# Products with the identity written as transposing instructions

## The reference

```
# block 1
h = concat(meta_tokens, x)                      # 272 rows
h = h + token_mixer(h)                          # "mixer 1": retention and mLSTM heads
h = h + expert_choice_ffn(h)                    # 16 experts of 1024 x 2816, 34 tokens each
x = rmsnorm(h)[16:]
# block 2; its context path depends on ctx alone, and only its end states are used
state_a, state_b = branches(ctx @ w_in)         # "the context"
oa = gdn_branch(a_lat, state_a)                 # "mixer 2": gated delta rule, chunks of 128, 4 heads, 2 directions
ob = rwkv_branch(b_lat, state_b)                # chunks of 64
y  = (sigmoid(g_a)*(oa @ w_o_a) + sigmoid(g_b)*(ob @ w_o_b)) @ w_out   # "the merge"
h  = x + m2 * y
h  = h + m5 * hier_moe(modulate(rmsnorm(h)))    # "the last block": 32 experts of 1024 x 256, top 2 of one group of 8
out = rmsnorm(h)
```

## Time and profile before

| | |
|---|---|
| median of 3 runs | 2938.16 us (2936.57 to 2940.39) |
| the profiled execution's own time | 2939.95 us |
| its span in the profile | 2938.2 us |
| PE busy | 2566.5 us (87%), 20619 records |
| weight loads (PEld) busy | 1431.2 us, 20619 records |
| DVE busy | 891.5 us (30%) |
| ACT busy | 415.4 us (14%) |
| HBM traffic | 268 GB/s over the span |

### The profile page before, as it was taken

The page is one execution under the profiler, slowest core; times in us unless marked ns, Lnnn a source line. Parts: engine busy times, 40 slices in busy tenths (PEclk is TensorE's granted clock), DMA queues, the critical chain, the costliest instruction groups (busy, mean ns, idle before and its releaser), DMA issues. The chain is left out here.

```text
span 2938.2 us, 45579 instructions
## 1 busy us (share of the span) xinstructions
PE 2566.5 (87%) x20619; PEld 1431.2 (49%) x20619; DVE 891.5 (30%) x1804; ACT 415.4 (14%) x826; POOL 85.3 (3%) x93
## 2 busy tenths in 40 slices
PE   6979579998999998999999999878676889779995
PEld 4524235334444433544444444346665888445553
DVE  1216732301212112131303131027538441242222
ACT  1022100100001000021202121013013221000001
POOL 0001000000000000000000000000000100000000
PEclk9987688999999999999999999989888989889997
DMA  5315335799999998999998999962010005259996
GB/s 178 115 57 192 124 134 216 285 409 386 399 381 375 388 416 350 364 381 403 386 392 360 378 406 394 378 255 93 1 37 1 3 32 190 106 237 423 422 422 277
DMA packets 129434, 789.27 MB, mean 269 GB/s; under 512 B 17473, under 2 KB 19785, under 8 KB 65113
## 3 DMA queue, kind: packets, MB, share of 16 engines
q1 hardware_dynamic: 125785, 773.78, 65.6%
q0 software_dynamic: 3456, 12.58, 1.1%
HBM read 774.79 MB, written 11.53 MB: 268 GB/s over the span
## 5 line engine op out<-in xcount | busy, mean ns | idle before, releaser
L3026 PE MATMUL bank<-ring,arena 128*34 128x512 f32 (+1 forms) x3072 | 692.5, 588 | 71.1 <-DMA ring<-in_w_up 52.7
L3026 PEld LDWEIGHTS bank<-ring,arena 128*34 128x34 f32 x3072 | 185.8, 116 | 477.6 <-issue 456.2
L3052 PE MATMUL bank<-ring,arena 128*34 128x512 f32 (+1 forms) x1536 | 339.4, 559 | 0.7 <-DVE arena L2032 0.7
L3052 PEld LDWEIGHTS bank<-ring,arena 128*34 128x34 f32 x1536 | 106.4, 112 | 184.4 <-issue 146.0
L303 PE MATMUL bank<-arena,ring 128*128 128x256 f32 (+1 forms) x688 | 159.2, 394 | 3.9 <-DVEq L2049 1.8
L303 PEld LDWEIGHTS bank<-arena,ring 128*128 128x128 f32 x688 | 134.1, 195 | 29.5 <-DVEq L2049 2.2
L3509 PE MATMUL bank<-ring,arena 128*64 128x256 f32 x992 | 111.1, 379 | 3.5 <-DMA ring<-in_moe_w_up 2.8
L2023 DVE TENSOR_TENSOR arena<-arena,bank 34x512 f32<-34x512 f32 (+3 forms) x112 | 59.2, 576 | 156.3 <-ACT arena L1095 155.4
L2924 PEld LDWEIGHTS bank<-arena 64*64 64x64 f32 x2304 | 75.7, 139 | 49.5 <-issue 49.5
L313 PE MATMUL bank<-ring,arena 128*128 128x512 f32 (+1 forms) x224 | 98.8, 596 | 0.0
L3038 PEld LDWEIGHTS bank<-consts,arena 34*64 34x64 f32 x1408 | 88.6, 216 | 13.8 <-issue 12.3
(11 more groups left out here) (634 smaller groups left out, 2959.8 us busy)
## 6 DMA issues: line engine op xcount, KB each, us to landing
ring<-in_w_gate SPq DMA_DIRECT2D x128, 1408.0 KB, 13.1
ring<-in_w_up SPq DMA_DIRECT2D x128, 1408.0 KB, 12.9
ring<-in_w_down SPq DMA_DIRECT2D x128, 1408.0 KB, 10.6
ring<-in_w_in SPq DMA_DIRECT2D x46, 1024.0 KB, 7.1
ring<-in_moe_w_down SPq DMA_DIRECT2D x33, 1024.0 KB, 15.4
ring<-in_moe_w_gate SPq DMA_DIRECT2D x31, 1024.0 KB, 13.6
ring<-in_moe_w_up SPq DMA_DIRECT2D x31, 1024.0 KB, 16.0
ring<-in_ada_w SPq DMA_DIRECT2D x24, 1024.0 KB, 7.3
```

The costliest lines, as they stand in the source:

```text
L3026: last = mm(ps[c][row:row + CAP, 0:n], xsT[:, e, k, :], w[:, at:at + n], start=k == 0, stop=k == KT - 1)
L3052: last = mm(ps[6][row:row + CAP, c:c + n], hidT[:, j, :], w[:, at - m * PIECE:at - m * PIECE + n], start=j == 0, stop=j == FT - 1)
```

## The change

Products of a whole stationary tile with the identity are written with `nc.tensor.transpose`. No instruction stands at another place on any engine: the order of PE's list is the same row for row, and waits and semaphores are the same.

- In the context: a new helper `turned_heads` turns k (8 products), v (8) and broadcasts beta (16); `vT7c` is turned with it directly (16).
- In mixer 2: the broadcast of beta (16 products, four in each of four groups of 16).
- In the merge: `row_of_columns_pe` (32 products).
- In the last block: the turn of the hidden rows, four products per pair with 64 rows each, two in the last pair (78 in all).

Products with the identity whose result goes to half of the partitions (lines 2855, 2962, 3038, 3205, 3279, 3326, 3454) stay as they are.

```diff
+                def turned_heads(dst, src):
+
+                    for h in range(4):
+                        last = nc.tensor.transpose(dst[:, h * P:(h + 1) * P], src(h), ident)
+                    return last
+
...
-                    heads(bank_a, lambda h: kT_c[:, h, c * P:(c + 1) * P], lambda h: ident).then_inc(turned, up(turned))
+                    turned_heads(bank_a, lambda h: kT_c[:, h, c * P:(c + 1) * P]).then_inc(turned, up(turned))
...
-                    heads(bank_a, lambda h: vT_c[:, h, c * P:(c + 1) * P], lambda h: ident).then_inc(turned, up(turned))
+                    turned_heads(bank_a, lambda h: vT_c[:, h, c * P:(c + 1) * P]).then_inc(turned, up(turned))
...
-                        token = for_dve(heads(bank_a, lambda h: beta_c[:, cs[d], 4 * d + h:4 * d + h + 1].to_broadcast([P, P]), lambda h: ident))
+                        token = for_dve(turned_heads(bank_a, lambda h: beta_c[:, cs[d], 4 * d + h:4 * d + h + 1].to_broadcast([P, P])))
...
-                        last = mm(bank_a[0:C7, q * P:(q + 1) * P], vT7c[:, q, c * C7:(c + 1) * C7], ident, start=True, stop=True)
+                        last = nc.tensor.transpose(bank_a[0:C7, q * P:(q + 1) * P], vT7c[:, q, c * C7:(c + 1) * C7], ident)
...
-                        mm(ps[b0 + 1][:, hs], beta[:, c, e:e + 1].to_broadcast([P, P]), ident, start=True, stop=True)
+                        nc.tensor.transpose(ps[b0 + 1][:, hs], beta[:, c, e:e + 1].to_broadcast([P, P]), ident)
...
-                    last = mm(ps[base + k // 4][:, k % 4 * P:(k % 4 + 1) * P], column(k).to_broadcast([P, P]), ident,
-                              start=True, stop=True)
+                    last = nc.tensor.transpose(ps[base + k // 4][:, k % 4 * P:(k % 4 + 1) * P], column(k).to_broadcast([P, P]), ident)
...
-                        last = mm(ps[4][:, f * P + m * CAP2:f * P + (m + 1) * CAP2], hid2_by2[0:CAP2, m, f, :],
-                                  ident[0:CAP2, 0:CAP2], start=True, stop=True)
+                        last = nc.tensor.transpose(ps[4][:, f * P + m * CAP2:f * P + (m + 1) * CAP2], hid2_by2[0:CAP2, m, f, :],
+                                                   ident[0:CAP2, 0:CAP2])
```

## The result

| | before | after |
|---|---|---|
| median of the runs | 2937.36 us (6 runs, 2932.77 to 2941.76) | 2921.32 us (6 runs, 2918.64 to 2930.32) |
| ratio | | 0.9944, interval 0.9926 to 0.9962 |
| span of the profiled execution (its own time) | 2938.2 (2939.95) | 2922.9 (2924.66) |
| PE busy, records | 2566.5 us, 20619 | 2541.2 us, 20445 |

The sign was forecast, the size was not: 6 us were expected and 2927.5 us was the lower end of the range.

The account below looks back on a forecast made before the run. PE is busiest but not the only bound: transfers bind the last block and parts of the context. Terms 2.25 + 1.8 + 1.25 + 0.75 = 6.05 us saved gave 2932.1 us from the 2938.16 median; range 2927.5 to 2938 us.

Parts of the forecast that it names:

- One replacement: Every changed place: one transpose record replaces a product's two, 0.226 us becoming 0.114, saving 0.112 us at full clock.
- rival 5: Broadcast-column or 64-row transposes cost as much as products; only 1.8 us of the context is kept: 2936.4 us, chance 0.07.
- Context: 48 products, 5.4 us of PE work; 2.25 us kept where DMA engines idle afterwards, ends 0 and 5.4.
- beta's and `vT7c`'s 3.15 us: Context: saving lost because full DMA follows: beta 0.9 and 0.45 us, `vT7c` 1.8 us.
- Rival 2: Context keeps nothing, idle DMA stretches being given back at the next wait: 3.8 us saved, 2934.4 us, chance 0.09.
- rival 3: More is kept: half of the context's lost 3.15 us and two more last-block pairs: 2929.5 us, chance 0.11.
- Mixer 2: 16 products ahead of DVE's first reader, eight per chunk, no transfer near: all 1.8 us kept.
- Merge: 32 products, 3.6 us of PE work; root then waits for DVE's variances, so 1.25 us kept, with a 2.5 us PE gap.
- rival 1: Clock falls in the merge's new gap, costing 1.7 us: 4.4 us saved in all, 2933.8 us, chance 0.25.
- Last block: 78 products, 9.7 us of PE work, nearly all lost to transfers; 0.75 us kept, in the first and last pairs.
- the eighth: Last block: waits for `in_moe_w_up` from about this pair on, PE's lead shrinking 0.95 us a pair instead of 0.45.
- Rival 4: Transposes keep the clock up less than products, 1.7 us per added half-clock stretch; slower from the fourth on; chance 0.08.

Follow-up runs that it names:

- e11_mixer2_half: Kernel before with every second of mixer 2's products for beta left out (8 of 16; half of the heads get a wrong beta): 2929.94 us, ratio 0.9976.
- e9_burst_transposes: Changed kernel with two long transpose bursts: merge's first row issued 40 times, router's first column 80 times; 2978.86 us, one execution.

## Why the prediction was wrong in size

- **One replacement** (0.226 to 0.114 us, one record for two) was right: the distances in the merge are (3.68 - 0.27) / 31 = 0.110 us. The broadcast and the 64-row forms go to one record too, and rival 5 is out. The factor is 2, not 4. A group of four with 64 rows takes 0.69 us in place of 1.15, a little less saved than the 0.5 us of the working.
- **Context**, forecast 2.25 us: here the step failed which called beta's and `vT7c`'s 3.15 us "lost" because the DMA engines are full right behind them. Doubling just those products cost 5.9 us of 7.2, where the forecast's reading gives 1 to 2, and over the 18 profiles a us of PE's time is worth 1.07 us of the segment. A full stretch of 30 us was not the bound where the share over the whole section is 0.93. The context alone gave 0.18%, 5.3 us, with a wide interval. Rival 2 (nothing kept) was the wrong way round, and rival 3, which let half of the 3.15 us back, was the nearest.
- **Mixer 2**, forecast 1.8 us "all of it": the records were right, the size was not, 6.2 us in the traces and 5 in the times. The working let the clock rise at the same moment as before and went no further than the group itself, so the step that failed is the clock's term behind it, put at nothing. The two bursts at 2073 and 2133 us, each behind 3.04 us of idleness and each with a half-clock part, were in the trace and were not read. e11_mixer2_half shows that the shorter PE work suffices. In the five profiles with the shorter work both bursts are always fast. In four of the 12 profiles with as much work as before one of the two is fast (145.5 to 147.6 us against 148.7), but in these the segment ahead (1911 to 2040 us) is 2.6 to 6 us longer. Taken together the two segments (1911 to 2189.6 us) are 278.0 to 279.1 us in 11 of the 12, 283.5 in the twelfth, and 272.2 to 274.7 in the five: the gain is near 6 us.
- **Merge**, forecast 1.25 us: 1.2 us, by the chain that was worked out, with the root behind line 2342. The gap is 2.65 us, and no profile with the changed merge shows a fall of the clock in it: rival 1 is false here. Not foreseen were the router's 2.5 us, about 140 us later, in a stage where the trace of before showed an unbroken 44.4 us at the half clock.
- **Last block**, forecast 0.75 us: 0.6 us by the segment, 1.2 us by the means over the profiles. That nearly all is lost was right, how it is lost was right in part. The waits for weights begin at 2813 us, in the fifteenth pair and not the eighth: PE's lead was to grow by 0.5 us more a pair, but 15 times PE waits up to 0.3 us for DVE's line 2512, and the distance from pair to pair fell from 15.65 us only to 15.49.
- **Rival 4** (slower by the clock) is false, by e9_burst_transposes.

In sum, the sum failed in two terms: the context's 3.15 us called lost, and the clock's part in mixer 2 and the router, put at nothing. PE's time that was kept is 5.4 + 1.8 + 1.2 + 0.6 = 9.0 us, where the forecast had 6.05; the clock gave 4.4 us in mixer 2 and 2.5 in the router, where the forecast had nothing. That is 15.9 us, beside 16.0 measured. The fit is closer than its terms, and in part luck: the context's part is known to 3 us at best, its 5.4 us is the forecast's own price for all 48 products, and the one pair of profiles shows 3.2 us there.

The failure in one sentence: saved time beside transfers was called lost by a reading of 30 us, and the clock had been treated only as a risk of the change (rivals 1 and 4), so that the range had no case for what a shift of 1 or 2 us can win through it.

## What to carry to other kernels

Before you call saved time lost to transfers, look at the DMA share over the whole section that the buffers span and not over the 30 us behind the edit: at 1.01 over 168 us about 1 of 9 us was kept, at 0.93 over 1360 us most of 5.4. These are two cases, not a threshold. List the bursts behind an edit that run partly at half the clock, and widen the range by what they could win; here that was worth more than the edit's own work in the same place (3.65 us in mixer 2's two bursts beside 1.8, and 2.5 in the router beside 1.2 in the merge). A segment that spreads from one execution to the next is to be read together with the one ahead of it. When a small edit gains more than its instructions, put their time back with the new instructions, and take it away with the old ones.

## What the runs showed of the hardware

- Float32 transposes held 2.4 GHz for 37 us by themselves, and a burst of them that began at 1.2 GHz reached 2.4 GHz 4.1 us after its start (products: 6.1 us, in one execution each).
- A float32 product with the identity is two records, the transposing instruction one, in all four forms seen: 128 by 128, a broadcast column, 64 columns and 64 rows.
- One and the same burst (96 records of 64x64 behind 3.04 us of idleness) took 3.1, 4.4 to 4.6 or 5.4 us over the 18 profiles. 32 records of 128x36 took 7.01, 4.46 to 4.50, 4.10 or 3.95 us behind 15.6 us of idleness and 16 transposes. What differs is where the stretches at the half clock fell.
- 1.8 us more of PE work in mixer 2 made its segment 0.3 us longer, and 1.8 us less made it 6.3 us shorter.
